# RWKV scan: the factors of a triangle's inverse applied to the right-hand side one by one, and the inverse of the diagonal blocks kept in one orientation

## The chip, the core and the metric

One core of one Trainium2 chip runs the whole program. The metric is the device time of one execution in microseconds (us), as the median of several executions. The inputs and all arithmetic are f32.

## What is computed

The program is a stack of blocks: feed-forward layers, an RWKV mixer, a convolution mixer and others. The change touches only the scan in the RWKV mixer. It runs over two sequences of 256 tokens (first the context, then the latent one, which starts from the context's final state), for 12 heads of 64 channels, forwards (d = 0) and backwards (d = 1):

```python
def wkv_scan(S0, r, w, k, v, kk, bb, reverse):
    def step(S, inp):
        rt, wt, kt, vt, kkt, bt = inp
        sk = jnp.einsum('bhij,bhj->bhi', S, kkt)
        S = S * wt[:, :, None, :] - sk[..., None] * bt[:, :, None, :] + vt[..., None] * kt[:, :, None, :]
        return S, jnp.einsum('bhij,bhj->bhi', S, rt)
    S, ys = lax.scan(step, S0, xs, reverse=reverse)
```

The kernel does this in chunks of 64 tokens. Inside a chunk the states are eliminated, and what is left is a triangular system (I + N) U = G per head and direction, where N is strictly triangular, 64 x 64. With U known, the new state and the outputs are plain products.

## The kernel before

Each sequence has CH = 4 chunks (n = 0 to 3, and 4 to 7 for the latent one). A chunk holds 24 matrices of 64 x 64 (12 heads, 2 directions). They lie as 6 pairs of heads q, and the pairs form NT = 2 halves t of three pairs each. Every buffer (a "unit") is 128 partitions x 768: partitions 0 to 63 are one head of each pair, 64 to 127 the other.

`products(t, s, turn, pairs)` (L663) issues one product for one half: 12 matmuls of 64 x 64, which the profile counts as 24 pairs of a weight load and a matmul, since each f32 matmul is two passes. With `turn=False` the two heads g of a pair are in rows g of TensorE's array and their results in partitions g; so only two of the four 64 x 64 quarters of the array ever work. With `turn=True` the result of head g and direction f goes to partitions f, so that all four quarters take turns. The result lands in one of two places s of the half's PSUM banks. `beside` (L683) and `first_b` (L697) are built like `turn=False`. `turned` (L714) transposes three 128 x 128 blocks.

The inverse of I + N is built in two levels. N is split by masks into its diagonal blocks of 8 x 8 (ND, and its transpose MD) and the rest (NO). The inverse D of the diagonal part comes from N2 = ND·ND, M2 its transpose, M4, P1 and a last product. Before, this last product is made twice, as DD and as its transpose DTR. Then E = D·NO is made in both orientations (EE, ETR), its square too (EE2, ET2), and its fourth power (ET4). The factors (I+E), (I+E2), (I+E4) are multiplied onto D one after the other: Q1 = ET4I·DD, Q2, TI. TI is the whole inverse. Beside that, GG, the right-hand side, is made of two products; UU = TI·GG; ST updates the state by two more, and Y (latent only) makes the output by three.

The order of the work is written out by hand, one list for each engine, in `rwkv_scan_pe` (L661), `rwkv_scan_act` (L906), `rwkv_scan_dve` (L1054) and `rwkv_scan_pool` (L1177). Each product's result is copied out of PSUM by ScalarE (ACT, L930) or VectorE (DVE, L1062, L1065), and each list counts its events: `e_pe.after(n, "GG")` is the count at which TensorE's product GG of chunk n is done. GpSimd (POOL) adds the identity to two factors (L1228).

The next chunk is prepared beside the present one. Its scaled keys KH and BH need this path: ACT makes exponentials into KH (`inverse_exps`, L926, two instructions per half), POOL turns them into BH and KH (`inverse_keys`, L1199 and L1200, four instructions per half), and then TensorE's `first_b` (L706) of the next chunk may start; `first_a` (`beside` with BH, L695) and the masks follow. ACT's exponentials overwrite KH, and POOL overwrites BH; so they come after KH and BH of the present chunk have been transposed by TensorE and copied out by ACT as KHT (L960) and BHT (L961).

Of the kernel before, what the change touches and what calls it, by code (L numbers as in the profile page):

```python
# [7 lines left out]
ALU = mybir.AluOpType  # L8
# [10 lines left out]
FT = FF // P  # L19
# [49 lines left out]
def constant_table():  # L69
# [36 lines left out]
    for name, sign, pick in (("strict", 1.0, lambda u: u), ("incl", 1.0, lambda u: u | eye), ("nincl", -1.0, lambda u: u | eye),  # L106
                             ("nblk", -1.0, lambda u: u & blk), ("noff", -1.0, lambda u: u & ~blk),
# [61 lines left out]
def build(nc, t, out, table_at, stop=None):  # L169

    stop = STOP if stop is None else stop
    with ExitStack() as ctx:
# [347 lines left out]
        e_act = Events([["M2", "P1", "DD", "EE", "EE2", "KBT", "VT", "GG", "UU1"]] * NCH)  # L520
# [3 lines left out]
        e_pool = Events([["KR", "KBH", "IMD", "VC", "ETI", "ET2I"]] * NCH)  # L524
# [26 lines left out]
        def scan_over(eng, seq):  # L551
            n = CH * (seq + 1) - 1
            for t in range(NT):
# [3 lines left out]
                eng.wait_ge(s_po[t], e_pool.after(n, "ET2I"))  # L557
# [103 lines left out]
        def rwkv_scan_pe(pe, mm, seq):  # L661
# [64 lines left out]
            for n in range(n0, n0 + CH):  # L726
# [2483 lines left out]
```

## Time and profile before

| what | us |
|---|---|
| median of 3 runs | 3001.93 |
| lowest and highest | 2997.94, 3005.49 |
| the profiled execution | 2999.04 |
| its span in the trace | 2997.2 |

The profile shows one execution. PE is TensorE's matmuls, PEld its weight loads, which overlap them; DVE, ACT and POOL are VectorE, ScalarE and GpSimd. A row of a timeline gives start, length, engine, line, operation, out<-in, a count, and in brackets how long the engine had been idle and what ended it. "issue" is a wait for nothing that the profile shows. The two scans lie at about 539 to 668 us and 770 to 922 us.

### The profile page before, as it was taken

Reading aid. Unit: us, or ns where it says so; the run is one execution under the profiler, and the core shown is the slowest. Engines: PE = TensorE matmul, PEld = TensorE weight load, DVE = VectorE, ACT = ScalarE, POOL = GpSimd, SP = SyncE. Lnnn points to the kernel's source line nnn. Section 1 sums busy time; section 2 is a strip of 40 time slices with the busy share of each in tenths; the row PEclk is TensorE's granted clock in tenths of the full one; section 3 lists DMA queues with packets and bytes.
Section 4 is the critical chain, followed back from the end, with each engine's and each line's share of the span. In section 5 each row is a group of like instructions: output and inputs, shape, how many; then the busy total and the mean of one; then the engine's idle time right before and its main releaser. Section 6 shows DMA issues by size and latency. Waiting matters only on the chain.

```text
span 2997.2 us, 62763 instructions
## 1 busy us (share of the span) xinstructions
PE 2854.1 (95%) x27428; PEld 2641.6 (88%) x27428; DVE 2059.0 (69%) x3587; ACT 583.4 (19%) x1319; POOL 306.7 (10%) x518
## 2 busy tenths in 40 slices
PE   7999998889889999999999999999999999998998
PEld 6888886777787999998899999978889989967998
DVE  6777636545564988995879889726259879853664
ACT  2000004333432201102220020033121021032101
POOL 0001002422440001000000100000000100000000
PEclk8999999999999999999999999999999999999999
DMA  7557313003004687786258868633457857722452
GB/s 281 169 180 243 123 46 109 4 24 108 31 4 156 213 280 252 228 280 216 91 192 267 295 202 277 198 113 113 141 191 259 295 176 260 262 79 86 141 190 92
DMA packets 387504, 514.54 MB, mean 172 GB/s; under 512 B 14032, under 2 KB 344976, under 8 KB 386080
## 3 DMA queue, kind: packets, MB, share of 16 engines
q1 hardware_dynamic: 347632, 366.73, 37.7%
q0 software_dynamic: 39456, 143.67, 13.9%
q8 instruction: 217, 3.56, 0.5%
q14 instruction: 55, 0.45, 0.0%
q10 hardware_dynamic: 144, 0.13, 0.0%
HBM read 509.44 MB, written 1.05 MB: 170 GB/s over the span
## 4 chain that ended last, share of the span: by engine, by line
PE 88%; DVE 5%; ACT 3%; DMA 2%; issue 2%; POOL 1%; SPq 0%; DVEq 0%; ACTq 0%; POOLq 0%
PE PS L2550 40%; PE PS L2608 20%; PE PS L656 6%; PE PS L676 5%; PE PS L833 3%; PE PS L1743 2%; PE PS L1668 2%; PE PS L2620 1%; PE PS L1519 1%; PE PS L2481 1%; PE PS L1425 1%; PE PS L2641 1%; PE PS L692 1%; DMA W<-in_e_w_in 0%; PE PS L2012 0%
## 5 line engine op out<-in xcount | busy, mean ns | idle before, releaser
L2550 PE MATMUL PS<-Y,W 128*128 128x128 f32 (+2 forms) x3536 | 483.7, 294 | 17.3 <-ACT Y L2747 13.1
L2550 PEld LDWEIGHTS PS<-Y,W 128*128 128x128 f32 x3536 | 453.2, 194 | 34.7 <-issue 16.0
L2608 PE MATMUL PS<-ARENA,W 128*128 128x128 f32 (+1 forms) x2816 | 362.3, 288 | 2.9 <-DVE ARENA L2887 1.6
L2608 PEld LDWEIGHTS PS<-ARENA,W 128*128 128x128 f32 x2816 | 346.3, 192 | 13.0 <-DVE ARENA L2887 2.0
L2811 DVE SCALAR_TENSOR_TENSOR ADAW<-ADAW,CB 128x1024 f32<-128x1024 f32 x280 | 332.6, 1220 | 0.6
L2452 POOL DMA_DIRECT2D ADAW<-in_ada_rows x272 | 144.4, 532 | 1829.7 <-DVE ADAW L2811 1486.8
L2550 PE MATMUL PS<-Y,ARENA 128*128 128x128 f32 (+2 forms) x2592 | 329.2, 282 | 2.2 <-DVE ARENA L2872 2.2
L2550 PEld LDWEIGHTS PS<-Y,ARENA 128*128 128x128 f32 x2592 | 312.7, 192 | 7.5 <-DVE ARENA L2872 3.0
L2550 PE MATMUL PS<-X,W 128*128 128x128 f32 x1920 | 234.4, 275 | 1.9 <-ACT JUNK L2709 1.9
L2550 PEld LDWEIGHTS PS<-X,W 128*128 128x128 f32 x1920 | 223.9, 192 | 2.7 <-ACT JUNK L2709 2.7
L2858 DVE TENSOR_TENSOR ARENA<-W 128x1024 f32<-128x1024 f32 (+1 forms) x120 | 159.3, 1327 | 10.0 <-DMA W<-in_ffn_w_down 4.2
L2867 DVE TENSOR_TENSOR W<-W 128x1024 f32<-128x1024 f32 (+1 forms) x120 | 159.0, 1325 | 0.0
L2863 DVE TENSOR_TENSOR ARENA<-ARENA,W 128x1024 f32<-128x1024 f32 (+1 forms) x116 | 152.5, 1315 | 0.3
L2608 PE MATMUL PS<-ARENA 128*128 128x128 f32 x1232 | 146.7, 275 | 0.0
L656 PE MATMUL PS<-Y,W 128*128 128x256 f32 (+2 forms) x560 | 129.0, 394 | 14.7 <-ACT Y L2747 13.1
L2608 PEld LDWEIGHTS PS<-ARENA 128*128 128x128 f32 x1232 | 142.1, 192 | 0.0
L676 PE MATMUL PS<-W 64*64 64x64 f32 x4608 | 115.2, 222 | 27.1 <-issue 24.1
L656 PEld LDWEIGHTS PS<-Y,W 128*128 128x128 f32 (+2 forms) x560 | 108.3, 194 | 35.3 <-issue 14.9
L676 PEld LDWEIGHTS PS<-W 64*64 64x64 f32 x4608 | 100.5, 134 | 39.4 <-issue 36.6
L2719 ACT ACTIVATE SIL<-SIL 128x256 f32<-128x256 f32 x73 | 30.4, 417 | 528.1 <-DVE SIL L3009 528.1
L833 PE MATMUL PS<-Y,W 128*128 128x256 f32 x528 | 122.5, 391 | 9.4 <-ACT Y L2747 4.6
L833 PEld LDWEIGHTS PS<-Y,W 128*128 128x128 f32 x528 | 101.7, 195 | 29.9 <-issue 13.4
(459 smaller groups left out, 4187.6 us busy)
## 6 DMA issues: line engine op xcount, KB each, us to landing
ADAW<-in_ada_rows POOLq DMA_DIRECT2D x272, 512.0 KB, 4.9
W<-in_ffn_w_gu SPq DMA_DIRECT2D x88, 1024.0 KB, 7.6
W<-in_ffn_in SPq DMA_DIRECT2D x88, 1024.0 KB, 7.6
W<-in_ffn_w_down SPq DMA_DIRECT2D x32, 1408.0 KB, 9.4
W<-in_ffn_out SPq DMA_DIRECT2D x32, 1408.0 KB, 9.2
W<-in_even_w_in SPq DMA_DIRECT2D x40, 512.0 KB, 4.6
W<-in_e_w_in SPq DMA_DIRECT2D x16, 512.0 KB, 4.6
W<-in_e_w_in SPq DMA_DIRECT2D x8, 1024.0 KB, 7.2
```

The costliest lines, as they stand in the source:

```text
L656: last = mm(PS[idx % 4][0:m_, 0:S], wide(c, kt, n_)[:, k, q * P:q * P + m_], x(k), start=(k == 0), stop=(k == kt - 1))
L676: last = mm(to, x, y, start=(k == 0), stop=(k == len(pairs) - 1))
L833: last_ = mm(PS[at[f] % 4][:, 0:S], w[:, k, q * P:(q + 1) * P], Y[:, k, off:off + S], start=(k == 0), stop=(k == DT - 1))
L1668: last = mm(PS[idx % 4][:, 0:S], wide(c, DT)[:, k, (i % 2) * P:(i % 2 + 1) * P], Y[:, k, 0:S], start=(k == 0), stop=(k == DT - 1))
L1743: last = mm(PS[idx % 4][:, 0:S], wide(c, 16)[:, k, (i % 2) * P:(i % 2 + 1) * P], Z16[:, k], start=(k == 0), stop=(k == 15))
L2452: pool.dma_start(ADAW[:, g % 2, i], t["ada_rows"][g * P:(g + 1) * P, i * D:(i + 1) * D])\
L2550: last = mm(block_bank(b, q, half), w[left][:, k, q * P:(q + 1) * P], yb[right][:, k], start=(k == 0 and p not in (2, 5)), stop=(k == 3), ...
L2608: last = mm(block_bank(b, 0, half), w[left][:, k], hb[right][:, k], start=(k == 0 and p not in (2, 5)), stop=(k == PAIRS - 1), skip_group_ ...
L2811: V.scalar_tensor_tensor(w, w, 1.0, CB[:, 0 if layer < 2 else 1], ALU.mult, ALU.mult, accum_out=MOD[:, layer, tile + i:tile + i + 1]).then ...
L2858: V.tensor_tensor(w["S1"], w["A21"], w["A22"], ALU.add).then_inc(s_s1, 1)
L2863: V.tensor_tensor(w["S2"], w["S1"], w["A11"], ALU.subtract).then_inc(s_s2, 1)
L2867: V.tensor_tensor(w["S3"], w["A11"], w["A21"], ALU.subtract).then_inc(s_s3, 1)
```

## The change

It takes products, copies and masks out of the scan and puts others in. All of it is inside the four lists; nothing outside the scan changes.

- The inverse D is made only as DD (`turn=True`). The off-diagonal mask is taken from the transposed product, as MO, in `first_b`'s step on DVE.
- F = MO·DD and its transpose FT take the place of EE and ETR; F2, FT2 and F4 are their powers, now with `turn=False`.
- The factors are no longer multiplied together. DG = DD·GG, then U1 = F4I·DG, U2 = F2I·U1, and UU = FI·U2. So Q1, Q2 and TI are gone, and DG, U1 and U2 are there, behind GG. GG itself has `turn=False`.
- KH is transposed behind GG, BH behind DG; both stood behind Q1 before, in one step. ACT copies them out after DG, and `inverse_exps` follows these copies.

```diff
-                             ("nblk", -1.0, lambda u: u & blk), ("noff", -1.0, lambda u: u & ~blk),
+                             ("nblk", -1.0, lambda u: u & blk), ("moff", -1.0, lambda u: u.T & ~blk),
...
-        PE_EV = ["N2", "M2", "M4", "P1", "DD", "DTR", "EE", "ETR", "EE2", "ET2", "ET4", "AKK", "Q1", "KBT", "Q2", "VT", "TI",
-                 "GG", "UU"]
-        DVE_EV = ["N2", "N2I", "M4I", "DTR", "ETR", "ET2", "ET4I", "AK", "Q1", "Q2", "TI"]
+        PE_EV = ["N2", "M2", "M4", "P1", "DD", "AKK", "F", "FT", "F2", "FT2", "F4", "VT", "GG", "KHT", "DG", "KBT", "U1",
+                 "U2", "UU"]
+        DVE_EV = ["N2", "N2I", "M4I", "AK", "F", "F2", "F4I", "U1", "U2"]
...
-        e_act = Events([["M2", "P1", "DD", "EE", "EE2", "KBT", "VT", "GG", "UU1"]] * NCH)
+        e_act = Events([["M2", "P1", "DD", "FT", "FT2", "VT", "GG", "VT1", "DG", "KBT", "UU1"]] * NCH)
...
                     pe.wait_ge(s_va[t], e_act.after(n, "P1"))
                     pe.wait_ge(s_vd[t], e_dve.after(n, "M4I"))
-                    products(t, 0, False, (M4, P1M)).then_inc(s_pp[t], 1)
-                    products(t, 1, True, (P1M, M4)).then_inc(s_pp[t], 1)
+                    products(t, 1, True, (M4, P1M)).then_inc(s_pp[t], 1)
+                    beside(t, 0, KH, n).then_inc(s_pp[t], 1)
                 for t in range(NT):
                     pe.wait_ge(s_va[t], e_act.after(n, "DD"))
-                    pe.wait_ge(s_vd[t], e_dve.after(n, "DTR"))
-                    products(t, 0, True, (DTR, NO)).then_inc(s_pp[t], 1)
-                    products(t, 1, True, (NO, DTR)).then_inc(s_pp[t], 1)
-                for t in range(NT):
-                    pe.wait_ge(s_va[t], e_act.after(n, "EE"))
-                    pe.wait_ge(s_vd[t], e_dve.after(n, "ETR"))
-                    products(t, 0, True, (ETR, EE)).then_inc(s_pp[t], 1)
-                    products(t, 1, True, (EE, ETR)).then_inc(s_pp[t], 1)
-                for t in range(NT):
-                    pe.wait_ge(s_va[t], e_act.after(n, "EE2"))
-                    pe.wait_ge(s_vd[t], e_dve.after(n, "ET2"))
-                    products(t, 0, True, (EE2, ET2)).then_inc(s_pp[t], 1)
-                    beside(t, 1, KH, n).then_inc(s_pp[t], 1)
-                for t in range(NT):
-                    pe.wait_ge(s_vd[t], e_dve.after(n, "ET4I"))
-                    products(t, 0, True, (ET4I, DD)).then_inc(s_pp[t], 1)
+                    products(t, 1, True, (MO, DD)).then_inc(s_pp[t], 1)
                     pe.wait_ge(s_vd[t], e_dve.after(n, "AK"))
-                    turned(t, 1, 0, KH)
-                    turned(t, 1, 1, BH).then_inc(s_pp[t], 1)
-                for t in range(NT):
-                    pe.wait_ge(s_vd[t], e_dve.after(n, "Q1"))
-                    pe.wait_ge(s_po[t], e_pool.after(n, "ET2I"))
-                    products(t, 0, True, (ET2I, Q1)).then_inc(s_pp[t], 1)
-                    pe.wait_ge(s_va[t], e_act.after(n, "KBT"))
+                    products(t, 0, True, (DD, MO)).then_inc(s_pp[t], 1)
+                for t in range(NT):
+                    pe.wait_ge(s_vd[t], e_dve.after(n, "F"))
+                    pe.wait_ge(s_va[t], e_act.after(n, "FT"))
+                    products(t, 1, False, (FT_, FF_)).then_inc(s_pp[t], 1)
+                    products(t, 0, False, (FF_, FT_)).then_inc(s_pp[t], 1)
+                for t in range(NT):
+                    pe.wait_ge(s_vd[t], e_dve.after(n, "F2"))
+                    pe.wait_ge(s_va[t], e_act.after(n, "FT2"))
+                    products(t, 0, False, (FT2, F2)).then_inc(s_pp[t], 1)
                     pe.wait_ge(s_po[t], e_pool.after(n, "VC"))
                     turned(t, 1, 0, VC).then_inc(s_pp[t], 1)
                 for t in range(NT):
-                    pe.wait_ge(s_vd[t], e_dve.after(n, "Q2"))
-                    products(t, 0, False, (ETI, Q2)).then_inc(s_pp[t], 1)
-                for t in range(NT):
-                    pe.wait_ge(s_vd[t], e_dve.after(n, "TI"))
+                    pe.wait_ge(s_vd[t], e_dve.after(n, "F4I"))
                     pe.wait_ge(s_va[t], e_act.after(n, "VT"))
-                    products(t, 0, True, (keys(n, 0), MST), (AK, VT0)).then_inc(s_pp[t], 1)
+                    products(t, 0, False, (keys(n, 0), MST), (AK, VT0)).then_inc(s_pp[t], 1)
+                    turned(t, 1, 1, KH).then_inc(s_pp[t], 1)
+                for t in range(NT):
+                    pe.wait_ge(s_va[t], e_act.after(n, "VT1"))
+                    products(t, 0, True, (DD, GG)).then_inc(s_pp[t], 1)
+                    turned(t, 1, 0, BH).then_inc(s_pp[t], 1)
+                for t in range(NT):
+                    pe.wait_ge(s_va[t], e_act.after(n, "DG"))
+                    products(t, 0, False, (F4I, DG)).then_inc(s_pp[t], 1)
+                for t in range(NT):
+                    pe.wait_ge(s_vd[t], e_dve.after(n, "U1"))
+                    pe.wait_ge(s_po[t], e_pool.after(n, "F2I"))
+                    products(t, 0, False, (F2I, U1)).then_inc(s_pp[t], 1)
                     if more:
+                        pe.wait_ge(s_va[t], e_act.after(n, "KBT"))
                         first_b(t, n + 1)
                 for t in range(NT):
-                    pe.wait_ge(s_va[t], e_act.after(n, "GG"))
-                    products(t, 0, False, (TI, GG)).then_inc(s_pp[t], 1)
+                    pe.wait_ge(s_vd[t], e_dve.after(n, "U2"))
+                    products(t, 0, False, (FI, U2)).then_inc(s_pp[t], 1)
                     if more:
                         first_a(t, n + 1)
...
-                    act.wait_ge(s_pp[t], e_pe.after(n, "DTR"))
-                    out(DD, t, 0).then_inc(s_va[t], 1)
-                for t in range(NT):
-                    act.wait_ge(s_pp[t], e_pe.after(n, "EE"))
-                    out(EE, t, 0).then_inc(s_va[t], 1)
-                for t in range(NT):
-                    act.wait_ge(s_pp[t], e_pe.after(n, "EE2"))
-                    out(EE2, t, 0).then_inc(s_va[t], 1)
+                    act.wait_ge(s_pp[t], e_pe.after(n, "DD"))
+                    out(DD, t, 1).then_inc(s_va[t], 1)
                 if more:
-                    for t in range(NT):
-                        exps(t, n + 1)
-                for t in range(NT):
-                    act.wait_ge(s_pp[t], e_pe.after(n, "KBT"))
-                    A(part(KHT, t), flat(t, 1, 0), ACT.Copy)
-                    A(part(BHT, t), flat(t, 1, 1), ACT.Copy, scale=-1.0).then_inc(s_va[t], 1)
-                for t in range(NT):
-                    if more:
-                        inverse_exps(t, n + 1)
+                    exps(0, n + 1)
+                for t in range(NT):
+                    act.wait_ge(s_pp[t], e_pe.after(n, "FT"))
+                    out(FT_, t, 0).then_inc(s_va[t], 1)
+                if more:
+                    exps(1, n + 1)
+                for t in range(NT):
+                    act.wait_ge(s_pp[t], e_pe.after(n, "FT2"))
+                    out(FT2, t, 0).then_inc(s_va[t], 1)
+                for t in range(NT):
                     act.wait_ge(s_pp[t], e_pe.after(n, "VT"))
-                    A(part(VT1, t), flat(t, 1, 0), ACT.Copy)
                     vt = flat(t, 1, 0).rearrange("p (q f e) -> p q f e", q=TQ, f=2)
                     for f in range(2):
                         for g in range(2):
@@ -973,6 +964,16 @@
                 for t in range(NT):
                     act.wait_ge(s_pp[t], e_pe.after(n, "GG"))
                     out(GG, t, 0).then_inc(s_va[t], 1)
+                    A(part(VT1, t), flat(t, 1, 0), ACT.Copy).then_inc(s_va[t], 1)
+                for t in range(NT):
+                    act.wait_ge(s_pp[t], e_pe.after(n, "DG"))
+                    out(DG, t, 0).then_inc(s_va[t], 1)
+                for t in range(NT):
+                    A(part(KHT, t), flat(t, 1, 1), ACT.Copy)
+                    act.wait_ge(s_pp[t], e_pe.after(n, "KBT"))
+                    A(part(BHT, t), flat(t, 1, 0), ACT.Copy, scale=-1.0).then_inc(s_va[t], 1)
+                    if more:
+                        inverse_exps(t, n + 1)
                 for t in range(NT):
...
             def first_b(t, n):
                 dve.wait_ge(s_pf[t], e_first.after(n, "B0"))
                 of = flat(t, 1).rearrange("p (q d e) -> p q d e", q=TQ, d=2)
+                V.tensor_tensor(cols4(MO)[:, qs(t)], of, mask("moff"), ALU.mult)
                 V.tensor_tensor(cols4(MD)[:, qs(t)], of, mask("mblk"), ALU.mult).then_inc(s_vf[t], 1)
             def first_a(t, n):
                 dve.wait_ge(s_pf[t], e_first.after(n, "A0"))
                 if lat:
-                    masked(ARB[n % 2], t, 1, "nincl")
-                masked(NO, t, 0, "noff")
-                masked(ND, t, 0, "nblk").then_inc(s_vf[t], 1)
+                    masked(ARB[n % 2], t, 1, "nincl", 1)
+                masked(ND, t, 0, "nblk", 1).then_inc(s_vf[t], 1)
...
                 for t in range(NT):
-                    dve.wait_ge(s_pp[t], e_pe.after(n, "DTR"))
-                    out(DTR, t, 1).then_inc(s_vd[t], 1)
-                for t in range(NT):
-                    dve.wait_ge(s_pp[t], e_pe.after(n, "ETR"))
-                    out(ETR, t, 1).then_inc(s_vd[t], 1)
-                for t in range(NT):
-                    dve.wait_ge(s_pp[t], e_pe.after(n, "ET2"))
-                    out(ET2, t, 1).then_inc(s_vd[t], 1)
-                for t in range(NT):
-                    dve.wait_ge(s_pp[t], e_pe.after(n, "ET4"))
-                    out_and_eye(ET4I, t, 0).then_inc(s_vd[t], 1)
                     dve.wait_ge(s_pp[t], e_pe.after(n, "AKK"))
                     if lat:
-                        masked(ARK, t, 1, "incl")
-                    masked(AK, t, 0, "strict").then_inc(s_vd[t], 1)
-                for t in range(NT):
-                    dve.wait_ge(s_pp[t], e_pe.after(n, "Q1"))
-                    dve.wait_ge(s_po[t], e_pool.after(n, "ETI"))
-                    out(Q1, t, 0).then_inc(s_vd[t], 1)
-                for t in range(NT):
-                    dve.wait_ge(s_pp[t], e_pe.after(n, "Q2"))
-                    out(Q2, t, 0).then_inc(s_vd[t], 1)
-                for t in range(NT):
-                    dve.wait_ge(s_pp[t], e_pe.after(n, "TI"))
-                    out(TI, t, 0).then_inc(s_vd[t], 1)
+                        masked(ARK, t, 1, "incl", 0)
+                    masked(AK, t, 0, "strict", 0).then_inc(s_vd[t], 1)
+                for t in range(NT):
+                    dve.wait_ge(s_pp[t], e_pe.after(n, "F"))
+                    out(FF_, t, 1).then_inc(s_vd[t], 1)
+                for t in range(NT):
+                    dve.wait_ge(s_pp[t], e_pe.after(n, "F2"))
+                    out(F2, t, 1).then_inc(s_vd[t], 1)
+                for t in range(NT):
+                    dve.wait_ge(s_pp[t], e_pe.after(n, "F4"))
+                    dve.wait_ge(s_po[t], e_pool.after(n, "FI"))
+                    out_and_eye(F4I, t, 0).then_inc(s_vd[t], 1)
...
+                for t in range(NT):
+                    dve.wait_ge(s_pp[t], e_pe.after(n, "U1"))
+                    out(U1, t, 0).then_inc(s_vd[t], 1)
+                for t in range(NT):
+                    dve.wait_ge(s_pp[t], e_pe.after(n, "U2"))
+                    out(U2, t, 0).then_inc(s_vd[t], 1)
...
-                for name, of, to in (("ETR", ETR, ETI), ("ET2", ET2, ET2I)):
+                for name, of, to in (("F", FF_, FI), ("F2", F2, F2I)):
```

TensorE's order, with its waits, in the first chunk. (W, ADAW, CB and CT are the large buffers in which the units lie; L676 is a product's matmul, L706 the one of `first_b`, L695 of `first_a`, L716 a transpose; x11 is 11 matmuls, each two passes.) First Q1 and the place of BH's transposes before:

```order
L676 MATMUL PS<-W 64x64 [waits scan_vector_read0]
L676 MATMUL PS<-W 64x64 x11
L716 MATMUL PS<-CT,W 128x128 [waits scan_vector_read0]
L716 MATMUL PS<-CT,W 128x128 x5
L676 MATMUL PS<-W 64x64 [waits scan_vector_read1]
L676 MATMUL PS<-W 64x64 x11
L716 MATMUL PS<-CT,W 128x128 [waits scan_vector_read1]
L716 MATMUL PS<-CT,W 128x128 x5
```

Q2 and TI of both halves and GG of half 0 follow before the first L706 of the next chunk. Now the same transposes (three of BH in a row of L716) and what follows, in the changed kernel:

```order
L676 MATMUL PS<-ADAW,W 64x64 [waits scan_scalar_read1]
L676 MATMUL PS<-ADAW,W 64x64 x11
L716 MATMUL PS<-CT,W 128x128 x3
L676 MATMUL PS<-ADAW,W 64x64 [waits scan_scalar_read0]
L676 MATMUL PS<-ADAW,W 64x64 x11
L676 MATMUL PS<-ADAW,W 64x64 [waits scan_scalar_read1]
L676 MATMUL PS<-ADAW,W 64x64 x11
L676 MATMUL PS<-W 64x64 [waits scan_pool_done0,scan_vector_read0]
L676 MATMUL PS<-W 64x64 x11
L706 MATMUL PS<-W 64x64 [waits scan_pool_done0,scan_scalar_read0]
L706 MATMUL PS<-W 64x64 x11
```

Between BH's last transposes and L706 of half 0 there are now U1 of both halves and U2 of half 0. L706 waits for POOL (KH and BH of the next chunk) and for ACT.

On ScalarE, the copies KHT and BHT and the exponentials, before (L960, L961, L926), stood ahead of the copies of V's transposes (L967, L971) and of GG (L930):

```order
L960 ACTIVATE ADAW<-PS 128x384 [waits scan_product_done0]
L961 ACTIVATE ADAW<-PS 128x384
L960 ACTIVATE ADAW<-PS 128x384 [waits scan_product_done1]
L961 ACTIVATE ADAW<-PS 128x384
L926 ACTIVATE W<-ARENA 128x3x64 x2
L967 ACTIVATE ADAW<-PS 128x384 [waits scan_product_done0]
L971 ACTIVATE ADAW<-PS 64x3x64 x4
L926 ACTIVATE W<-ARENA 128x3x64 x2
```

In the changed kernel they are L972, L974 and L924 and stand behind both copies of DG (the first two rows), just ahead of the copies of UU:

```order
L928 ACTIVATE ADAW<-PS 128x384 [waits scan_product_done0]
L928 ACTIVATE ADAW<-PS 128x384 [waits scan_product_done1]
L972 ACTIVATE ADAW<-PS 128x384
L974 ACTIVATE ADAW<-PS 128x384 [waits scan_product_done0]
L924 ACTIVATE W<-ARENA 128x3x64 x2
L972 ACTIVATE ADAW<-PS 128x384
L974 ACTIVATE ADAW<-PS 128x384 [waits scan_product_done1]
L924 ACTIVATE W<-ARENA 128x3x64 x2
```

What moved: the next chunk's exponentials now stand behind ACT's copies of V, GG and DG, and not ahead of them.

## Rows read from the trace of the kernel before

**Rows 1.** The page: the head, its first table, and the chain by line.

```profile
span 2997.2 us, 62763 instructions
PE 2854.1 (95%) x27428; PEld 2641.6 (88%) x27428; DVE 2059.0 (69%) x3587; ACT 583.4 (19%) x1319; POOL 306.7 (10%) x518
...
PE PS L2550 40%; PE PS L2608 20%; PE PS L656 6%; PE PS L676 5%; PE PS L833 3%; PE PS L1743 2%; PE PS L1668 2%; PE PS L2620 1%; PE PS L1519 1%; PE PS L2481 1%; PE PS L1425 1%; PE PS L2641 1%; PE PS L692 1%; DMA W<-in_e_w_in 0%; PE PS L2012 0%
```

**Rows 2.** Busy time by stretch: chunk 1's two parts, then the two scans.

```profile
core 0: us, PE busy (x) PEld busy (x) DVE busy (x) ACT busy (x) POOL busy (x), PEclk, DMA share, GB/s
572.30:589.40 17.10, 12.19 (x549) 11.31 (x549) 8.77 (x16) 6.32 (x18) 4.65 (x6) 1.00 0.02 4
589.40:605.10 15.70, 14.69 (x525) 13.30 (x525) 8.55 (x16) 8.06 (x22) 9.09 (x17) 1.00 0.02 4
541.90:668.00 126.10, 106.11 (x4202) 96.61 (x4200) 66.58 (x124) 54.88 (x148) 45.48 (x72) 1.00 0.02 4
774.00:922.00 148.00, 129.02 (x4726) 119.47 (x4722) 93.03 (x196) 57.80 (x160) 54.65 (x82) 1.00 0.02 4
```

**Rows 3.** Timeline of PE, the first part of chunk 1.

```profile
574.68 3.00 PE L676 MATMUL PS<-W 64*64 64x64 f32 x126 [0.84 <-issue]
...
582.10 2.39 PE L676 MATMUL PS<-W 64*64 64x64 f32 x127 [0.97 <-issue]
585.65 1.71 PE L676 MATMUL PS<-W 64*64 64x64 f32 x82 [1.16 <-issue]
```

**Rows 4.** DMA queues from 572.3 to 604.9 us: packets, MB, share.

```profile
q8 instruction: 8, 0.13, 1.7%
```

**Rows 5.** Timeline of PEld, the second part of chunk 1, and the start of chunk 3.

```profile
592.08 0.64 PEld L716 LDWEIGHTS PS<-CT,W 128*128 128x128 f32 x6
...
593.39 0.31 PEld L716 LDWEIGHTS PS<-CT,W 128*128 128x128 f32 x3
...
596.43 0.21 PEld L676 LDWEIGHTS PS<-CB,W 64*64 64x64 f32 x8
...
597.12 0.80 PEld L706 LDWEIGHTS PS<-W 64*64 64x64 f32 x24
...
599.84 0.83 PEld L676 LDWEIGHTS PS<-ADAW 64*64 64x64 f32 x24
600.54 0.83 PEld L695 LDWEIGHTS PS<-W 64*64 64x64 f32 x24
...
602.68 0.82 PEld L676 LDWEIGHTS PS<-ADAW 64*64 64x64 f32 x48
...
605.14 0.98 PEld L676 LDWEIGHTS PS<-W 64*64 64x64 f32 x30 [0.24 <-issue]
...
637.16 1.53 PEld L676 LDWEIGHTS PS<-W 64*64 64x64 f32 x49 [0.25 <-issue]
```

**Rows 6.** Timeline of ACT in chunk 1: KHT, BHT, exponentials, VT1, VT0.

```profile
591.68 0.49 ACT L960 ACTIVATE ADAW<-PS 128x384 f32<-128x384 f32 x1 [3.34 <-PE PS L716]
592.06 0.48 ACT L961 ACTIVATE ADAW<-PS 128x384 f32<-128x384 f32 x1
...
593.75 0.62 ACT L926 ACTIVATE W<-ARENA 128x192 f32<-128x192 f32 x2
594.26 0.50 ACT L967 ACTIVATE ADAW<-PS 128x384 f32<-128x384 f32 x1
594.63 1.33 ACT L971 ACTIVATE ADAW<-PS 64x192 f32<-64x192 f32 x4
```

**Rows 7.** Timeline of POOL in chunk 1: keys of halves 0 and 1, then identity.

```profile
594.45 0.59 POOL L1199 TENSOR_TENSOR W<-ARENA,W 128x192 f32<-128x192 f32 x1 [3.56 <-ACT W L926]
...
596.68 0.60 POOL L1199 TENSOR_TENSOR W<-ARENA,W 128x192 f32<-128x192 f32 x1
...
598.88 1.01 POOL L1205 TENSOR_TENSOR W<-W,CT 128x384 f32<-128x384 f32 x1
```

**Rows 8.** Groups of instructions from 541 to 670 us: copies and waits.

```profile
L1062 DVE COPY W<-PS 128x384 f32<-128x384 f32 x48 | 26.7, 557 | 32.5 <-PE PS L676 31.7
L930 ACT ACTIVATE W<-PS 128x384 f32<-128x384 f32 x40 | 19.4, 491 | 48.9 <-PE PS L676 48.9
```

**Rows 9.** Waits from 541 to 670 us: us, times, longest.

```profile
PEld PS L676 <- issue: 24.6, 49, 1.6
```

More of the change, by code:

```diff
@@ L470, in build @@
         KH, BH, VC = unit(4), unit(5), unit(6)
-        MD, ND, NO, IMD, M4I, N2I, ET2I = [unit(7 + i) for i in range(7)]
-        TI, GG, UU0, UU1, KHT, BHT, VT0, VT1, AK, ARK = [unit(14 + i) for i in range(10)]
+        MD, ND, MO, IMD, N2, N2I, F2I = [unit(7 + i) for i in range(7)]
+        M4, GG, UU0, UU1, KHT, BHT, VT0, VT1, AK, ARK = [unit(14 + i) for i in range(10)]
         MST, ARB_A = unit(24), unit(25)
         ARB = [ARB_A, SIL[:, :, :].rearrange("p a b -> p (a b)")[:, 0:UNIT]]
-        N2, M2, P1M = M4I, ND, MD
-        M4, DD, DTR, EE, ETR, ETI, EE2, ET2, ET4I, Q1, Q2 = TI, M4I, ND, MD, IMD, N2I, ND, NO, MD, IMD, ND
+        M2, P1M = ND, MD
+        DD, FF_, FT_, FI, F2, FT2, F4I, DG, U1, U2 = ND, MD, IMD, N2I, N2, MO, MD, M4, IMD, N2
         def kr4(n):
@@ L523, in build @@
         e_exp = Events([["E12", "E3"]] * NCH)
-        e_pool = Events([["KR", "KBH", "IMD", "VC", "ETI", "ET2I"]] * NCH)
+        e_pool = Events([["KR", "KBH", "IMD", "VC", "FI", "F2I"]] * NCH)
         s_mix = sem("mixer_weights_loaded")
@@ L556, in scan_over @@
                 eng.wait_ge(s_va[t], e_act.after(n, "UU1"))
-                eng.wait_ge(s_po[t], e_pool.after(n, "ET2I"))
+                eng.wait_ge(s_po[t], e_pool.after(n, "F2I"))
         FRONT = [([18, 6, 7], [8, 9, 10, 11, 12, 13], [14, 15, 16, 17]),
@@ L749, in rwkv_scan_pe @@
-                    products(t, 0, True, (DTR, NO)).then_inc(s_pp[t], 1)
-                    products(t, 1, True, (NO, DTR)).then_inc(s_pp[t], 1)
+                    products(t, 1, True, (MO, DD)).then_inc(s_pp[t], 1)
+                    pe.wait_ge(s_vd[t], e_dve.after(n, "AK"))
+                    products(t, 0, True, (DD, MO)).then_inc(s_pp[t], 1)
                 for t in range(NT):
-                    pe.wait_ge(s_va[t], e_act.after(n, "EE"))
-                    pe.wait_ge(s_vd[t], e_dve.after(n, "ETR"))
@@ L758, in rwkv_scan_pe @@
-                    pe.wait_ge(s_vd[t], e_dve.after(n, "ET2"))
-                    products(t, 0, True, (EE2, ET2)).then_inc(s_pp[t], 1)
-                    beside(t, 1, KH, n).then_inc(s_pp[t], 1)
-                for t in range(NT):
-                    pe.wait_ge(s_vd[t], e_dve.after(n, "ET4I"))
-                    products(t, 0, True, (ET4I, DD)).then_inc(s_pp[t], 1)
-                    pe.wait_ge(s_vd[t], e_dve.after(n, "AK"))
-                    turned(t, 1, 0, KH)
-                    turned(t, 1, 1, BH).then_inc(s_pp[t], 1)
@@ L975, in rwkv_scan_act @@
                     out(GG, t, 0).then_inc(s_va[t], 1)
+                    A(part(VT1, t), flat(t, 1, 0), ACT.Copy).then_inc(s_va[t], 1)
[6 more added lines that the diff above has]
+                    A(part(BHT, t), flat(t, 1, 0), ACT.Copy, scale=-1.0).then_inc(s_va[t], 1)
+                    if more:
+                        inverse_exps(t, n + 1)
                 for t in range(NT):
@@ L1066, in out_and_eye, with masked @@
                                        eye.unsqueeze(1).unsqueeze(1).to_broadcast([P, TQ, 2, HD]), ALU.add)
-            def masked(dst, t, which, name):
-                return V.tensor_tensor(cols4(dst)[:, qs(t)], outs_beside(t, 1)[:, :, :, which], mask(name), ALU.mult)
+            def masked(dst, t, which, name, s):
+                return V.tensor_tensor(cols4(dst)[:, qs(t)], outs_beside(t, s)[:, :, :, which], mask(name), ALU.mult)
             def first_b(t, n):
```

3 lines of the change are left out of this document (1 added, 2 removed).

## The prediction

> **What bounds the kernel now.** I read the page first. Its chain gives TensorE 88% of the span, but L676, the scan's product line, only 5% [rows 1]. So the change can move only the two scans, some 280 us. The busy time by stretch shows how they differ from the rest: the clock stands at its full 2.4 GHz level (1.00), and yet TensorE is busy 106.1 of 126.1 us in the first scan and 129.0 of 148.0 in the second, with DVE, ACT and POOL far below it [rows 2]. No engine is full; something comes between.
>
> The waits and the timeline say what. PEld stands 24.6 us in front of L676 with no releaser ("issue"), 49 times [rows 9]. In the timeline these pauses come after pieces of 126 or 127 matmuls, 0.84 to 1.16 us each [rows 3]; that is about 254 instructions with the weight loads. The instruction queue moves 8 packets of 16 KB each in one chunk [rows 4], and a chunk has 549 + 525 = 1074 pairs of weight load and matmul [rows 2], or 8.5 pieces. So I read the pauses as TensorE waiting for its instructions: a piece lasts at least some 3.6 us (from 582.10 to 585.65 [rows 3] it is 3.55), however fast its matmuls are. In the chunk's first part 549 pairs take 17.1 us, 31.1 ns a pair, and TensorE is busy 12.2 of it [rows 2]. In the second part it waits less, and TensorE's own pace and the copies set the time.
>
> A page of the Trainium skill says the contrary ("Runtime: NRT & Kernel Launch", section on instruction fetch): blocks of 256 instructions are fetched while the last ones run, and the cost is mostly hidden, since engines issue more slowly than blocks arrive. The block size agrees with the pieces of 126 to 127 pairs; the hiding does not agree with the pauses of 0.84 to 1.16 us. By that rule the sum below would lose its cover for the slower products; it is the rival D.
>
> **What products cost.** Weight loads start at even distances, so the price is read from start to start. GG (`turn=True`, 48 pairs): 596.43 to 597.12, 14.4 ns a pair, 0.35 us for a product of one half. UU (`turn=False`): 599.84 to 600.54, 29.2 ns a pair, 0.70 us. Three transposes take 0.32 us (six take 0.64) [rows 5]. So `turn=False` costs twice as much.
>
> **The change, counted.** Before, a context chunk makes 19 products per half, 5 of them `turn=False` (N2, M2, DD, TI, UU); after, 18, of which 10 (N2, M2, F2, FT2, F4, two in GG, U1, U2, UU). The latent chunks have three more in both. TensorE's own time per chunk goes up by 10 x 0.70 less 12 x 0.35, that is 2.8 us (five more slow products and six fewer fast ones, two halves). Pairs go down by 48, to 1026. DVE loses two copies per half, ACT gains one and POOL keeps its two additions: a copy is 0.56 us on DVE and 0.49 on ACT [rows 8], beside TensorE's other half, so they count only where a product waits for them. MO's mask takes the place of NO's: nothing, both engines being idle much of the time [rows 2].
>
> **The new wait.** BH is now transposed behind DG, and everything that prepares the next chunk hangs on it. I count from the end of half 0's transposes of BH (time 0).
> - ACT: its copy of DG, half 1, comes first. That product ends at about 0.6 (it waits 0.3 for VT1), and its copy at 1.35. Then KHT and BHT, 0.4 each (591.68 to 592.06), to 2.15, and two exponentials, 0.6: 2.8 [rows 6].
> - POOL: four instructions for half 0 take 2.23 (594.45 to 596.68), for half 1 again 2.2 (to 598.88) [rows 7]. With 0.1 to start, BH of the next chunk is ready at 5.1 and 7.35.
> - TensorE: transposes of half 1 to 0.95, U1 of both halves 1.40, 0.27 for DVE's copy of U1, U2 of half 0 0.70: it reaches L706 at 3.3. It waits to 5.2, about **2.0 us**. L706 (0.70) and U2 of half 1 (0.70) bring it to 6.6; it waits to 7.4, another **0.8 us**.
>
> Behind that wait, in TensorE's queue, stand U2 of half 1 and UU, the path to the new state, so nothing covers it. The price is 2.85 us (2.0 and 0.8, the roundings kept) for each of 6 steps from a chunk to the next, three per sequence: 17.1 us. Before, the same exponentials began at 593.75 [rows 6], and POOL was done with half 0 at 596.7 [rows 7] when L706 began at 597.12 [rows 5]: with little to spare, but on time.
>
> **The sum for one chunk.** After, from the first matmul of GG: GG 1.40 and KH's transposes 0.32, twice; DG 0.35 and BH's 0.32, 0.27, and the same again; U1 1.40; 0.27; U2 0.70; wait 2.0; L706 0.70; U2 0.70; wait 0.84; L706 0.70; UU and L695 for both halves 2.80. That is 15.2 us, and from ST to the next chunk's N2 2.46 as before (602.68 to 605.14 [rows 5]): 17.6. The rest of the chunk, N2 to F4, is 1026 less 492 = 534 pairs. Its own pace would be about 12.5 us, so the supply of instructions still sets it; at the 31.1 ns a pair of before it is 16.6. GG then waits 0.7, because VT0's four copies take 1.33 [rows 6] and only F4 and V's transposes of half 1 (1.02) lie beside them, less the time to start. Sum: 34.9 us. Before, chunk 1 took 32.8 (N2 at 572.3 [rows 2] to 605.14) and chunk 2 took 32.0 (605.14 to 637.16) [rows 5], 32.4 on average. So +2.5 for each of 6 chunks, 15.0. The last chunk of each sequence has no next one to wait for: 2.5 - 2.85 = -0.35, twice, -0.7. In the latent chunks L692, Y and the masks are the same in both, so I use the same difference. **Total +14.3 us.** The profiled execution took 2999.0, so 3013.3 for it; the median stands 2.9 above it, so **3016 us**.
>
> Ends of the unknown costs: the wait could be shorter by 0.6 us per chunk if POOL's first keys begin as soon as ACT's first exponential is out (-4). The 31.1 ns a pair holds where half the products are fast; with F2, FT2 and F4 slow, three products of both halves are 2.1 us more of TensorE's own time, of which up to half may show, 1.0 us on 8 chunks (+8). With the difference taken against 32.8 instead of 32.4 it is 3 less. So 3006 to 3026 where this case holds.
>
> **Rivals.**
> - B, faster: the supply of instructions bounds all of the scan, the second part too, and the preparation is hidden (ACT or POOL run 2.8 us ahead of my count). Then only the 48 pairs per chunk count: 384 x 31.1 ns = 11.9 us less, 2990. For it: the pauses [rows 3, 9]. Against it: in the second part TensorE is busy 14.7 of 15.7 us [rows 2], so a slow product shows there.
> - C, no change: the wait for L706 is hidden, but the slower products are not. 14.3 - 17.1 = -2.8, so 2999. It decides if BH is ready within 3.3 us of its transposes. Against it: POOL's four instructions alone take 2.23.
> - D, slower still: the pauses are not a supply that covers anything (the skill's rule). Then 2.8 us for 8 chunks, 22.4, and the wait, 17.1, are both seen: about 3041. Against it: the pauses and their distance.
> - That the change doesn't do what it says: the counts from the program's order are as told, so I give that nothing.
>
> **How the numbers follow.** My forecast has 0.74, B 0.06, C 0.13, D 0.07. About 0.3%, 9 us, is what a measurement of this kernel can tell from no change. Slower by more than that: the forecast's part above 3011 (0.67 of its 0.74) and D, 0.74. Within: C and the forecast's low end, 0.20. Faster: B, 0.06. The range takes the forecast's own 3006 to 3026 and reaches down to take in a part of C: 3002 to 3027.
>
> **What the profile of the changed kernel should show.** TensorE idle before L706 with POOL's L1196 as releaser, about 2.0 and 0.8 us, in 6 chunks. A chunk of some 35 us in the first scan instead of 32.4. Pauses of about 1 us still every 126 to 127 pairs from N2 to F4, and fewer behind. Wrong if L706 follows U2 without a wait (C), or if chunks last over 37 us while the waits are as told (D).

## The result, and the profile after

| | before | after |
|---|---|---|
| median, us (5 runs each) | 3001.47 | 3018.85 |
| lowest and highest | 2997.94, 3005.49 | 3016.7, 3022.2 |
| span of the profiled execution | 2997.2 | 3020.4 |
| both scans, us | 270.1 | 285.5 |

The ratio is 1.0059, with a 95% interval of 1.0044 to 1.0073: 17.4 us slower, where 14.3 were forecast. The last line is read from the timeline of DVE, start to start: from the first N2I addition of a sequence (half 0; L1095 before, L1096 after) to its last state addition (half 1; L1151, L1147), both sequences added. It is free of what the rest of the program does from run to run, and I use it beside the ratio below, but it comes from one execution of each kernel. It rose by 15.4 us, so the change's cost lies in the scans.

Two parts of a chunk are used below. The head runs from N2I to the first weight load of GG, the tail from there to the next chunk's N2I. The tail repeats closely: it took 19.41, 19.42 and 19.41 us in the context's three steps of the changed kernel, and 10.3 to 10.7 before. What varies are the heads: the kernel before, e6 and e8 have the same head, and their sums over the six steps are 129.0, 126.8 and 130.1 us. So a difference of up to some 3 us between two values of "both scans" tells nothing by itself, and the tail is the sharper measure.

Busy time by stretch after, for chunk 1 from N2 to GG and from GG to the next N2, and for the two scans:

```profile
core 0: us, PE busy (x) PEld busy (x) DVE busy (x) ACT busy (x) POOL busy (x), PEclk, DMA share, GB/s
578.50:596.30 17.80, 14.30 (x534) 13.22 (x534) 8.65 (x16) 7.49 (x22) 6.20 (x8) 1.00 0.02 5
596.30:614.20 17.90, 15.62 (x492) 14.08 (x492) 6.55 (x14) 7.54 (x20) 7.58 (x14) 1.00 0.01 3
543.80:681.40 137.60, 116.42 (x4008) 106.24 (x4004) 57.97 (x107) 57.90 (x156) 45.96 (x72) 1.00 0.02 4
787.50:940.00 152.50, 138.65 (x4513) 129.03 (x4510) 84.43 (x178) 60.12 (x167) 54.66 (x82) 1.00 0.02 4
```

The counts are the forecast's: 534 pairs, then 492. The first part took 17.8 us, the second 17.9, where 17.3 and 17.6 had been worked out. Before, with its parts cut elsewhere, the same chunk took 32.8 [rows 2]. The timeline of PE shows the pauses that answer to [rows 3]:

```profile
585.43 0.74 PE L695 MATMUL PS<-W 64*64 64x64 f32 x19 [1.22 <-issue]
588.98 3.38 PE L676 MATMUL PS<-W 64*64 64x64 f32 x127 [0.78 <-issue]
593.28 1.15 PE L676 MATMUL PS<-W 64*64 64x64 f32 x32 [0.93 <-issue]
```

They are still there, 125 to 128 pairs of the records apart. That they are waits for instructions can be read from the trace too, which holds every packet of the instruction queue. Before, PE has 26 pauses over 0.4 us with "issue" as releaser in the two scans, and 25 of them end 1.2 to 1.5 us after a 16 KB packet has landed; after, it has 17, and all of them end so. They stand in the heads; no tail of either kernel has one.

The new wait, in the timeline of PEld, ACT and POOL around the end of chunk 1:

```profile
600.97 0.31 PEld L716 LDWEIGHTS PS<-CT,W 128*128 128x128 f32 x3
...
604.01 0.78 PEld L676 LDWEIGHTS PS<-W 64*64 64x64 f32 x24
606.28 0.81 PEld L706 LDWEIGHTS PS<-W 64*64 64x64 f32 x24 [1.49 <-issue]
...
608.47 0.81 PEld L706 LDWEIGHTS PS<-W 64*64 64x64 f32 x24 [0.69 <-issue]
```

```profile
602.10 0.49 ACT L928 ACTIVATE ADAW<-PS 128x384 f32<-128x384 f32 x1 [0.49 <-PE PS L676]
602.48 0.48 ACT L972 ACTIVATE ADAW<-PS 128x384 f32<-128x384 f32 x1
602.85 0.50 ACT L974 ACTIVATE ADAW<-PS 128x384 f32<-128x384 f32 x1
603.22 0.63 ACT L924 ACTIVATE W<-ARENA 128x192 f32<-128x192 f32 x2
```

```profile
603.93 0.59 POOL L1195 TENSOR_TENSOR W<-ARENA,W 128x192 f32<-128x192 f32 x1 [8.17 <-ACT W L924]
...
606.12 0.59 POOL L1195 TENSOR_TENSOR W<-ARENA,W 128x192 f32<-128x192 f32 x1
```

BH's transposes of half 0 end at 601.3. ACT copies DG of half 1 from 602.10 on, then KHT, BHT and the exponentials; POOL starts at 603.93 and is done with half 0 at about 606.2. TensorE is through with U2 of half 0 (start 604.01, 0.70 long) at 604.71 and begins L706 at 606.28: 1.57 us of wait. For half 1 it is 0.80. The list of waits for the whole first scan shows it on both queues of TensorE, and on PE it names the releaser, POOL's L1196; for the second scan the same two lines stand again:

```profile
PEld PS L706 <- issue: 6.5, 6, 1.5
PE PS L706 <- POOL W L1196: 5.9, 6, 1.4
```

### The profile page after: what moved, and what is told of

It is laid out like the page before. It is cut to its first block, busy times and chain, and to the rows that moved or that the text cites. A ratio compares the mean times of both kernels' runs of the same rounds, so it can differ in the third digit from the quotient of the medians.

```text
span 3020.4 us, 61959 instructions
## 1 busy us (share of the span) xinstructions
PE 2877.7 (95%) x27044; PEld 2662.4 (88%) x27044; DVE 2041.5 (68%) x3555; ACT 589.0 (19%) x1335; POOL 306.2 (10%) x518
## 4 chain that ended last, share of the span: by engine, by line
PE 87%; DVE 5%; DMA 3%; ACT 3%; issue 1%; POOL 1%; SPq 0%; DVEq 0%; ACTq 0%; POOLq 0%
PE PS L2546 39%; PE PS L2604 20%; PE PS L656 6%; PE PS L676 5%; PE PS L831 3%; PE PS L1739 2%; PE PS L1664 2%; PE PS L2616 1%; PE PS L1515 1%; DMA W<-in_ffn_out 1%; PE PS L2477 1%; PE PS L692 1%; PE PS L1421 1%; PE PS L2637 1%; PE PS L716 1%
## 5 line engine op out<-in xcount | busy, mean ns | idle before, releaser
L2715 ACT ACTIVATE SIL<-SIL 128x256 f32<-128x256 f32 x73 | 30.4, 417 | 533.3 <-DVE SIL L3005 533.3
L676 PE MATMUL PS<-W 64*64 64x64 f32 x4224 | 121.2, 220 | 11.4 <-issue 8.4
L676 PEld LDWEIGHTS PS<-W 64*64 64x64 f32 x4224 | 111.8, 135 | 18.0 <-issue 15.4
```

The lines of the kernel that those rows point to most:

```text
L676: last = mm(to, x, y, start=(k == 0), stop=(k == len(pairs) - 1))
```

## The experiments

Every run is compared with the kernel before on the same chip. "Scans" is the last line of the table above, and the last column is the mean tail of the context's and of the latent scan's three steps.

| run | made from | ratio to before, interval | scans, us | tail, us |
|---|---|---|---|---|
| before | | | 270.1 | 10.6, 16.6 |
| after | | 1.0059, 1.0044 to 1.0073 | 285.5 | 19.4, 25.0 |
| e1_early_keys | after | 1.0015, 1.0005 to 1.0025 | 272.3 | 17.5, 23.1 |
| e2_head_turned | after | 1.0030, 1.0019 to 1.0041 | 280.3 | 19.4, 25.4 |
| e3_fast_twice | before | 1.0031, 1.0019 to 1.0044 | 279.8 | 10.9, 16.5 |
| e4_slow_twice | before | 1.0032, 1.0022 to 1.0042 | 278.3 | 10.7, 16.5 |
| e5_keys_and_turned | after | 0.9993, 0.9984 to 1.0002 | 263.9 | 17.2, 22.9 |
| e6_late_exps | before | 1.0059, 1.0041 to 1.0078 | 287.1 | 14.0, 19.6 |
| e7_five_turned | after | 1.0052, 1.0038 to 1.0066 | 285.5 | 21.0, 26.4 |
| e8_slow_gg | before | 1.0007, 0.9995 to 1.0019 | 273.3 | 11.1, 16.5 |
| e9_reordered | after | 0.9976, 0.9966 to 0.9986 | 263.5 | 16.9, 22.1 |
| e10_fast_gg | after | 1.0023, 1.0012 to 1.0034 | 275.3 | 18.1, 23.9 |

**e1: the wait taken away.** In ACT's list, for half 0 (half 1 follows behind DG's copies), and in POOL's:

```diff
                     A(part(VT1, t), flat(t, 1, 0), ACT.Copy).then_inc(s_va[t], 1)
+                    if t == 0:
+                        act.wait_ge(s_pp[t], e_pe.after(n, "KHT"))
+                        A(part(KHT, t), flat(t, 1, 1), ACT.Copy)
+                        if more:
+                            inverse_exps(t, n + 1)
...
                 pool.wait_ge(s_ex[t], e_exp.after(n, "E3"))
+                if n > CH * seq:
+                    pool.wait_ge(s_pp[t], e_pe.after(n - 1, "KBT"))
```

> The changed kernel, with ACT's copy of KHT and the exponentials of half 0 moved ahead of the copies of DG, those of half 1 right behind them, and POOL itself waiting for BH's transposes. My theory (the late preparation of the next chunk is the price): TensorE's waits before first_b, measured in the changed kernel at 1.57 and 0.80 us from start to start, go from all 6 steps between chunks, 14.2 us less than the changed kernel, about 3005. Rival (the slower, later products set the end, and the wait only covers them): less than 5 us is gained, 3014 or more.

Measured: 1.0015 where the change had 1.0059, 13 us less, and the scans 13.2 less. My expectation held, and the rival is out. U2's loads of a half are 0.70 us long; L706 of half 0 follows them at once, that of half 1 after 0.17:

```profile
601.33 0.78 PEld L676 LDWEIGHTS PS<-W 64*64 64x64 f32 x24
602.02 0.78 PEld L706 LDWEIGHTS PS<-W 64*64 64x64 f32 x24
602.73 0.78 PEld L676 LDWEIGHTS PS<-W 64*64 64x64 f32 x24
603.60 0.81 PEld L706 LDWEIGHTS PS<-W 64*64 64x64 f32 x24
```

Every tail is 1.9 to 2.0 us shorter, some 12 us in the six steps, and the heads, which have the same products, make up the rest. So the late preparation is 12 to 13 of the change's 17 us.

**e2: the head's products fast.**

```diff
-                    products(t, 1, False, (FT_, FF_)).then_inc(s_pp[t], 1)
-                    products(t, 0, False, (FF_, FT_)).then_inc(s_pp[t], 1)
+                    products(t, 1, True, (FT_, FF_)).then_inc(s_pp[t], 1)
+                    products(t, 0, True, (FF_, FT_)).then_inc(s_pp[t], 1)
...
-                    products(t, 0, False, (FT2, F2)).then_inc(s_pp[t], 1)
+                    products(t, 0, True, (FT2, F2)).then_inc(s_pp[t], 1)
```

> The changed kernel, with F2, FT2 and F4 issued with turn=True (their results then lie in other places, so the output is not the reference's; the instructions are as many). TensorE's own time falls by 2.1 us a chunk, 16.8 in all. My theory (this part of a chunk is paced by the supply of instructions): at most a quarter of it shows, 0 to 4 us less than the changed kernel. Rival D (nothing is hidden by the pauses): 17 us less.

Measured: the scans 5.2 us less, 31% of the 16.8; by the ratios it is 8.7 us, about half, with some 5 us of doubt either way. Neither expectation, though nearer to mine: half to two thirds of the slow pace is hidden, not three quarters or more. The tails of the first scan stayed at 19.4, as they should.

**e3 and e4: what a pair costs in the head.** In the kernel before, one product is issued twice, a fast one or a slow one. (The fast one is EE2, the square that is made of EE and ETR, and not EE as the expectation calls it; both are `turn=True`.)

```diff
+                    products(t, 0, True, (ETR, EE))
                     products(t, 0, True, (ETR, EE)).then_inc(s_pp[t], 1)
```

```diff
+                    products(t, 0, False, (M4, P1M))
                     products(t, 0, False, (M4, P1M)).then_inc(s_pp[t], 1)
```

> The kernel before, with the product EE (turn=True) issued twice in each half of each chunk: 384 pairs of weight load and matmul more, 5.6 us of TensorE's own time at 14.4 ns a pair. Supply theory: 31.1 ns a pair, 11.9 us more than before, about 3013. Rival (own pace alone): 5.6 us more, 3007.

> The kernel before, with the product DD (turn=False) issued twice: again 384 pairs more, but 11.2 us of TensorE's own time at 29.2 ns a pair. Supply theory: a pair costs the same here as in the run with the fast product, about 12 us more than before. Rival (own pace): twice the price of the fast product's run.

Measured: 1.0031 and 1.0032; the scans 9.7 and 8.2 us longer. A fast pair costs as much as a slow one, though its own time is half: 384 pairs at 25 and 21 ns. By TensorE's own pace the slow product should have cost 5.6 us more than the fast one; it cost 1.5 less by the scans and 0.3 more by the ratios. Taken alone, neither price is far from its own pace, given the doubt in the heads and the intervals; the pair of runs is what tells. Both prices are under the 31.1 ns. The waits of the first scan show how it comes about. From the 24.6 us of [rows 9] they grew by 2.0 with the fast product and fell by 2.6 with the slow one, whose longer work fills them:

```profile
PEld PS L676 <- issue: 26.6, 46, 1.8
```

```profile
PEld PS L676 <- issue: 22.0, 45, 1.5
```

**e6: the wait made in the kernel before.** Nothing but the exponentials' place is changed:

```diff
-                    if more:
-                        inverse_exps(t, n + 1)
                     act.wait_ge(s_pp[t], e_pe.after(n, "VT"))
...
+                if more:
+                    for t in range(NT):
+                        inverse_exps(t, n + 1)
                 for t in range(NT):
                     act.wait_ge(s_pp[t], e_pe.after(n, "GG"))
```

> The kernel before, with nothing changed but the place of ACT's exponentials for the next chunk: behind the copies of V's transposes of both halves instead of ahead of each. POOL then ends half 1 about 3.4 us later than before. My theory (a wait there is covered by nothing): 3.4 us for each of 6 steps, 20 us more than before. Rival (UU, ST and the state's update have slack of their own): under 10 us more.

Measured: the scans 17.0 us longer, the ratio as the change's own. PEld in chunk 1 waits 3.21 us before L706:

```profile
601.44 0.77 PEld L706 LDWEIGHTS PS<-W 64*64 64x64 f32 x23 [3.21 <-POOL W L1201]
```

The granted clock is also at the lower level in three stretches inside these scans, 10.2 us in all, so the 17.0 us alone would not do as proof. But the tails without such a stretch are longer by 3.2 us in the first scan (13.77, twice) and by 2.8 in the second (19.44 and 19.43), where 3.4 were expected. So a wait at this place is nearly all paid, in the old kernel too.

**e7: faster products in front of the wait.** e2's edit, and U1 and U2 as well; the layouts then swap back, so that the output is computed in full again.

```diff
-                    products(t, 0, False, (F4I, DG)).then_inc(s_pp[t], 1)
+                    products(t, 0, True, (F4I, DG)).then_inc(s_pp[t], 1)
...
-                    products(t, 0, False, (F2I, U1)).then_inc(s_pp[t], 1)
+                    products(t, 0, True, (F2I, U1)).then_inc(s_pp[t], 1)
```

> The changed kernel with F2, FT2, F4, U1 and U2 with turn=True, and the late keys as they are. My theory (the keys' path from BH's transposes sets when L706 runs): U1 and U2 being faster buys nothing in the 6 steps between chunks, the wait before L706 grows by what they save, 1.57 to about 2.6 us; only the last chunk of each sequence gains 1.4. So 2 to 3 us less than e2. Rival (the products' own time counts): 11 us less than e2.

Measured: 1.0052, the scans 285.5, that is 5.2 us more than e2. The rival is out, but my 2 to 3 us of gain did not come either. The wait grew from 1.57 to 2.2 us and not to 2.6, since U2 now waits 0.47 us for DVE's copy of U1. What I had not foreseen is in the widths of the rows behind it:

```profile
605.13 0.77 PEld L706 LDWEIGHTS PS<-W 64*64 64x64 f32 x23 [2.15 <-issue]
...
607.33 1.39 PEld L706 LDWEIGHTS PS<-W 64*64 64x64 f32 x24 [1.04 <-issue]
```

24 pairs take 1.39 us instead of 0.8: the clock had fallen. Busy time by stretch shows the granted clock, the column behind POOL (a mean over the stretch), at 0.60 behind the wait and 0.53 in an earlier stretch:

```profile
593.50:596.80 3.30, 3.05 (x51) 2.63 (x49) 0.29 (x1) 1.82 (x6) 0.01 (x1) 0.53 0.00 0
596.80:605.00 8.20, 6.00 (x184) 4.83 (x180) 1.58 (x3) 5.26 (x14) 2.21 (x5) 1.00 0.01 4
605.00:607.30 2.30, 1.26 (x48) 1.16 (x48) 0.82 (x2) 0.00 (x0) 2.22 (x5) 0.91 0.00 0
607.30:611.00 3.70, 3.64 (x80) 3.67 (x81) 1.69 (x4) 0.49 (x1) 1.96 (x3) 0.60 0.02 4
```

**e8 and e10: GG's pace.** GG alone, slow in the kernel before (e8), fast in the changed one (e10).

```diff
-                    products(t, 0, True, (keys(n, 0), MST), (AK, VT0)).then_inc(s_pp[t], 1)
+                    products(t, 0, False, (keys(n, 0), MST), (AK, VT0)).then_inc(s_pp[t], 1)
```

> The kernel before, with GG alone issued with turn=False as in the change (its result lies elsewhere, so the output is not the reference's): 48 slow pairs for 48 fast ones in each half, 1.4 us of TensorE's own time a chunk, 11.4 in all. My theory (behind GG the tail runs at TensorE's own pace): all of it shows, 11 us more than before. Rival (supply covers it here as well): 0 to 3 us.

Measured: 1.0007, the scans 3.2 us longer. The expectation failed; about the rival's 0 to 3 us came. In the kernel before, GG of half 1 waits 0.53 us, for ACT's copies of V (on PE the releaser of this wait is L971), and L706 and UU then follow at once. These are its rows, from the kernel before:

```profile
598.45 0.24 PEld L676 LDWEIGHTS PS<-CB,W 64*64 64x64 f32 x8 [0.53 <-issue]
...
599.14 0.83 PEld L706 LDWEIGHTS PS<-W 64*64 64x64 f32 x24
```

A slower GG of half 0 fills this wait first. In e8 the slow GG of half 1 starts without one:

```profile
598.57 0.31 PEld L676 LDWEIGHTS PS<-CB,W 64*64 64x64 f32 x8
...
599.96 0.78 PEld L706 LDWEIGHTS PS<-W 64*64 64x64 f32 x24
600.66 0.32 PEld L676 LDWEIGHTS PS<-CB,W 64*64 64x64 f32 x8
```

Of the 1.4 us a chunk, 0.5 shows in the context's tails (11.1 for 10.6) and nothing in the latent's. Where the rest went beyond this wait I did not trace.

> The changed kernel with GG alone issued with turn=True (its result lies elsewhere, so the output is not the reference's). In the kernel before, GG's pace was hidden by ACT's copies of V and POOL's keys (e8). In the changed kernel nothing but V's copy of half 1 stands beside GG, and the keys' path begins behind it: of the 1.4 us a chunk, 0.3 is taken back by that copy, so 1.1 us in 8 chunks, 8.5 us less than the changed kernel. Rival (ACT's copies hide GG here as well): 0 to 2 us less.

Measured: 1.0023, the scans 10.2 us less than the change's. In the changed kernel GG is paid, as expected: the tails are 1.3 and 1.1 us shorter, where 1.1 had been said. The same edit costs 0 to 0.5 us a chunk in one kernel and gives 1.1 to 1.3 in the other.

**e5 and e9: a better version.** e5 is e1's edit and e7's together. e9 is e5, and moves `first_b` of half 1 behind UU of half 0 (L706 of half 0 stays where it was):

```diff
                     products(t, 0, False, (FI, U2)).then_inc(s_pp[t], 1)
+                    if more and t == 0:
+                        pe.wait_ge(s_va[1], e_act.after(n, "KBT"))
+                        first_b(1, n + 1)
                     if more:
                         first_a(t, n + 1)
```

> The changed kernel with the early keys of e1 and with F2, FT2, F4, U1 and U2 all issued with turn=True. Their layouts then swap and swap back, so that the result is the same as the changed kernel's. From e1 (17.6 less 14 over before), the head's three products give some 5 to 8 us as in e2; U1 and U2 save 1.4 us a chunk, 11 in all, of which POOL's keys of half 1 (ready 4.65 us after BH's transposes, TensorE there at 3.7) take back about 1.0 in 6 steps. Expected: 12 us less than e1, about 9 us less than the kernel before. Rival (the tail's pace is not TensorE's own): no gain from U1 and U2, 5 to 8 us less than e1.

> The kernel of e5, with first_b of half 1 moved behind UU of half 0. In e5 TensorE stood 1.19 us before it in each step (start to start). UU of half 0 (0.70 us) now fills part of that wait: 0.7 us in 6 steps, 4 us less than e5, so about 6 us less than the kernel before. Rival (DVE's masks behind first_b then set the end): the same as e5.

Measured: e5 0.9993, the scans 8.4 us less than e1's and 6.2 less than before's; by the ratios 6.6 and 2.1 less, and e5 is not told apart from the kernel before. That is not my 12 us less than e1 but the rival's 5 to 8. The tails say why: 17.2 and 22.9 us, only 0.2 less than e1's, so the fast U1 and U2 give next to nothing in the six steps. TensorE now waits 1.0 us a chunk for POOL in front of L706 of half 1, as foreseen, and 0.47 for DVE's copy of U1 in front of U2, which I had left out. The waits of e5's first scan:

```profile
PE PS L706 <- POOL W L1204: 3.0, 3, 1.0
PEld PS L676 <- DVE W L1069: 2.2, 5, 0.5
```

e9: 0.9976, the scans 263.5. Its move works as expected in five of six tails, which are 0.5 to 0.9 us shorter than e5's, but its heads are 2.0 us longer in sum, and the scans differ by 0.4 us, the ratios by 5 us with intervals that touch. So that e9 beats e5 is not shown. But e9 beats the kernel before by 0.24% (interval 0.14 to 0.34), and the change as it was by some 25 us.

## Why the prediction was right

- **The wait before L706.** The path was as told: BH's transposes, ACT, POOL, L706. It measured 1.57 and 0.80 us, 2.37 instead of 2.85, since ACT's copies and exponentials start 0.37 us apart and POOL could start 2.6 us after the transposes instead of 2.9. e1 and e6 show from both sides that it is paid. Taking it away gave 13.2 us in 6 steps, or 2.2 each, of which 1.9 to 2.0 are in the tails.
- **The supply of instructions.** The pauses stayed, they end with the landing of a packet of instructions, and e3 and e4 show one price for a fast and a slow pair. The sum let them hide all of the slower pace in the head and its upper end half; they hide half to two thirds (e2). N2 to GG took 17.8 us instead of 17.3.
- **The tail behind GG.** It took 17.9 us for 17.6, with two errors that cancel: a shorter wait, and a longer rest. The terms as they are listed add up to 15.4, not 15.2, unless DVE's 0.27 behind DG is counted once; with 15.4 the forecast would have been 2 us higher.
- **The base.** I took 32.4 us for a chunk before. From N2I to N2I the context's chunks took 30.4, 32.8 and 32.0, after 34.7, 35.7 and 35.5, so 3.6 each instead of 2.5. Chunk 0 was not in the average, and it is the shortest before.
- **The latent scan.** "I use the same difference" was wrong: its chunks took 37.9, 38.8, 38.6 and then 38.7, 40.1, 40.0, so 1.2 each. Its tail grew as much as the context's (8.4 us against 8.9, from GG to the next N2I), but its head shrank more, from 21.8 to 14.5 us against 21.2 to 15.9. The traces show where: PE's pauses over 0.3 us with no releaser sum to 3.2 us a head before and 0.7 after in the latent's steps, against 3.3 and 2.9 in the context's. Why the pauses went there and not here stays open.
- **The last chunks** lost 0.2 and 1.1 us instead of gaining 0.35.

In sum 10.7 us in the context's three steps, 3.5 in the latent's, 1.3 in the last chunks: 15.5 instead of 14.3. The forecast's own parts were 7.5, 7.5 and -0.7. So the mechanism, a wait that is paid in six steps and slower products that are mostly hidden in the head, is what happened; that the total came within 1.2 us by the scans, and 3 us by the medians, is partly luck, since errors of +3.2, -4.0 and +2.0 us cancel. The range was not fully worked out either: the ends named, -4, -3 and +8 around 3016, give 3009 to 3024 and not 3006 to 3026.

The rivals: B and C needed the wait hidden, and it was seen. D is out by its size, 3041, and by e2, where 17 us should have come and 5 to 9 did. D went by the rule of the Trainium skill ("Runtime: NRT & Kernel Launch", instruction fetch) that fetching is mostly hidden. Here that agrees with the tails, which have no such pause, and not with the heads, which pause for 3.3 us a chunk before and 2.9 after in the first scan; there, pairs that take TensorE 5.6 and 11.2 us cost the same 8 to 10 (e3, e4).

## What to carry to other kernels

When a step of preparation for the next round is moved, count its whole path from the event that now frees it to the instruction that waits, on each engine, and compare that with what is left in front of the waiting instruction. Products made faster in front of such a wait buy nothing (e7), and where the wait is gone they run into the next one (e5). And where very short matmuls come thick, count instructions as well as busy time; but look at each product's neighbours before pricing its pace, since the same edit was worth 0 to 0.5 us a chunk in one order and 1.1 to 1.3 in the other. When executions differ by several us, compare a stretch that repeats, as the tails do here.

## What the runs showed that I had not expected

- **The clock falls inside the scan when the waits grow.** In e7 the granted clock stood at the lower level (1.2 GHz) in seven stretches of 3.4 to 6.8 us in the two scans, 27 us in all. In e6, with waits of 3.2 and 0.7 us, it did so in three stretches, in e2 in one; in the kernel before, in the change itself and in all other runs in none, from the first N2I to the last state addition of either scan. At that level the 24 weight loads of a slow product took 1.39 us instead of 0.8. In e7 the seven stretches lie in tails, but for the first 1 us of one: against the change's 19.4 and 25.0 us, the four tails with one stretch of 3.4 us are longer by 0.4 to 1.3, the two with twice as much by 2.4 and 2.6. That is more than the 5.2 us by which e7 lies above e2, so the clock can account for it and for the gain that did not come. What exactly makes the clock fall, the length of a wait or the work around it, no run here separates.
- **Supply costs less than its average.** The 31.1 ns a pair were taken from chunk 1, whose pauses sum to 4.8 us, where the eight chunks before have 3.3 on average; a pair added costs 21 to 25 ns. A piece of 127 pairs in 3.55 us would be 28. What makes up the rest was not traced.
